# Five FFN pairs with seven block products in place of eight for half of their depth

## What is computed

```python
def swiglu(h, w_ffn_in, w_ffn_out):
    gate, up = jnp.split(h @ w_ffn_in, 2, axis=-1)
    return (jax.nn.silu(gate) * up) @ w_ffn_out
...
        x = x + gate2 * swiglu(h, w_ffn_in[l], w_ffn_out[l])
```

## Time and profile before

| | us |
|---|---|
| median of 3 runs | 3431.92 (3427.52 to 3432.31) |
| profiled execution | 3425.8 |
| its span | 3424.1 |
| TensorE busy | 2587.7 (76%) |
| VectorE busy | 2513.7 (73%) |
| GpSimd busy | 1102.7 (32%) |
| ScalarE busy | 860.9 (25%) |

### The profile page before, as it was taken

The page is one execution under the profiler, slowest core; times in us unless marked ns, Lnnn a source line. Parts: engine busy times, 40 slices in busy tenths (PEclk is TensorE's granted clock), DMA queues, the critical chain, the costliest instruction groups (busy, mean ns, idle before and its releaser), DMA issues. The chain is left out here.

```text
span 3424.1 us, 27357 instructions
## 1 busy us (share of the span) xinstructions
PE 2587.7 (76%) x10431; PEld 1805.0 (53%) x10431; DVE 2513.7 (73%) x2615; ACT 860.9 (25%) x815; POOL 1102.7 (32%) x654
## 2 busy tenths in 40 slices
PE   9999999616051500035558999999999999999999
PEld 4455774202020200012226888788788788888887
DVE  5987657899999999976776876779566544444565
ACT  2113331100000110000003333455433433333333
POOL 6640007686777688876660000000000000000000
PEclk9999999757575755567779999999999999999999
DMA  8885569999999999999997997455657555555775
GB/s 287 320 315 205 183 243 406 403 422 419 422 421 417 409 420 422 422 421 421 422 421 260 327 323 260 145 162 166 221 185 252 167 194 184 192 187 188 269 266 185
DMA packets 317685, 1023.39 MB, mean 299 GB/s; under 512 B 33656, under 2 KB 34184, under 8 KB 250892
## 3 DMA queue, kind: packets, MB, share of 16 engines
q1 hardware_dynamic: 243676, 484.97, 41.2%
q0 software_dynamic: 73904, 537.04, 37.9%
HBM read 1015.08 MB, written 6.86 MB: 298 GB/s over the span
## 5 line engine op out<-in xcount | busy, mean ns | idle before, releaser
L411 DVE TENSOR_TENSOR slab_low<-ring,slab_high 128x2048 fp32r<-128x2048 f32 x220 | 504.2, 2292 | 488.3 <-ACT slab_high L404 488.2
L404 ACT CAST slab_high<-ring 128x2048 fp32r<-128x2048 f32 x284 | 542.3, 1910 | 890.8 <-PE bank L390 714.7
L2137 POOL DMA_INDIRECT pool<-in_peer_u,pool x237 | 493.8, 2084 | 293.5 <-DVE pool L1861 185.9
L1911 DVE CUSTOM_DVE_ANT_0 pool<-pool,nat 128x2048 f32<-128x2048 f32 x234 | 532.7, 2291 | 45.7 <-DMA pool<-in_peer_u,pool 44.2
L388 PE MATMUL bank<-slab_high,left_high 128*128 128x512 f32 x1408 | 551.3, 392 | 8.4 <-DVE res L1949 3.9
L390 PE MATMUL bank<-slab_high,left_low 128*128 128x512 f32 x1408 | 549.0, 390 | 0.0
L389 PE MATMUL bank<-slab_low,left_high 128*128 128x512 f32 x1408 | 548.8, 390 | 0.0
L2710 PE MATMUL bank<-pool,causal 128*128 128x512 f32 x296 | 181.5, 770 | 415.7 <-ACT causal L2352 325.4
L1922 DVE SCALAR_TENSOR_TENSOR res<-pool,res 128x2048 f32<-128x2048 f32 x169 | 397.4, 2351 | 105.9 <-DMA pool<-in_peer_v,pool 92.5
L2137 POOL DMA_INDIRECT pool<-in_peer_v,pool x242 | 394.9, 1632 | 214.0 <-PE bank L2710 107.7
L2710 PE MATMUL bank<-pool,upto 128*128 128x512 f32 x288 | 195.9, 844 | 209.2 <-DMA pool<-in_peer_v,pool 116.3
(11 more groups left out here) (661 smaller groups left out, 3466.1 us busy)
## 6 DMA issues: line engine op xcount, KB each, us to landing
ring<-in_w_in SPq DMA_DIRECT2D x140, 1024.0 KB, 5.2
ring<-in_w_ffn_in SPq DMA_DIRECT2D x88, 1024.0 KB, 5.0
ring<-in_w_ffn_out SPq DMA_DIRECT2D x44, 1024.0 KB, 5.2
nat<-in_w_ada SPq DMA_DIRECT2D x74, 512.0 KB, 5.8
ring<-in_w_out SPq DMA_DIRECT2D x32, 1024.0 KB, 5.1
ring<-in_w_ada SPq DMA_DIRECT2D x28, 1024.0 KB, 6.7
left_scratch<-in_w_ada SPq DMA_DIRECT2D x38, 512.0 KB, 5.7
pool<-in_w_ada SPq DMA_DIRECT2D x12, 1024.0 KB, 7.1
```

The costliest lines, as they stand in the source:

```text
L404: nc.scalar.copy(high[:, n % PARTS], ring[:, g % SLOTS]).then_inc(high_done, 1)
L411: eng.tensor_tensor(dst, ring[:, g % SLOTS], high[:, n % PARTS].bitcast(F32), ALU.subtract)\
L1911: v.tensor_tensor_reduce(out=row, in0=row, in1=nat[:, t, :], scale=1.0, scalar=0.0, op0=ALU.mult, op1=ALU.add, accum_out=actv[:, t, m:m + ...
L2137: g.indirect_dma_start(dst, None, a[table][0], bass.IndirectOffsetOnAxis(idx[:, t, n:n + 1], 0))\
```

## The change

In pairs 1 to 5 the slabs 2 and 3 of the gates and of the ups are taken together. They are a matrix of 2 by 2 blocks (depth chunk 2 or 3, gate or up columns), as are the tokens (tile 0 or 1, depth chunk 2 or 3). The eight block products, 12 matmuls each, become seven by Strassen's scheme with sums of blocks on both sides (Winograd's form, with shared sums). The first two slabs of gates and ups (`rest`) stay as they are and now come behind the seven.

- *Left sums*, once: in pair 0 GpSimd makes four sums of 128x512 from the rows of `nat` (`left_sums`), TensorE turns them (16 transposes), ScalarE and VectorE make the two parts.
- *Weight sums*, each pair: GpSimd makes four sums of 128x2048 in place in the ring (`slab_sums`), each waiting for the one before.
- *Products*: in the order ONE, TWO, THREE, FIVE, SIX, FOUR, SEVENTH, with three part buffers in turn (a third one is added). ONE, TWO, THREE use slabs as loaded; FIVE, SIX, FOUR and SEVENTH use sums 1, 3, 4 and 2.
- *Recombination*: ScalarE takes banks 6 and 7 (ONE, FIVE) to SBUF, VectorE adds in six instructions of 128x512 that read a bank each, GpSimd makes two differences of 128x512 in SBUF, and silu and product work on SBUF tiles (`seven_silu`, `seven_product`).
- *Loads*: each pair still loads eight slabs; first the four for the seven products, then the four rest slabs into the slots in the order 0, 2, 1, 3, when low parts and sums have read them.

Some semaphores of earlier phases are reused in place of new ones, with their counts carried on; these waits are otherwise the same. The core of the diff (the loads and loops of pairs 0 and 6 to 10 do as before):

```diff
+        SEVEN = range(1, 6)
+        tail = 4 * SEVEN.stop * T
...
+        summed_rows = [nat[:, t, n * NB:(n + 1) * NB] for t, n in ((0, 0), (0, 1), (1, 0), (0, 3))]
+        s_wh, s_wl, s_wu = sem("seven_high_parts"), sem("seven_low_parts"), sem("seven_products")
+        s_ws, s_wx, s_wd = sem("slab_sums"), sem("seven_banks_taken"), sem("seven_banks_added")
+        ONE, TWO, THREE, FIVE, SIX, FOUR, SEVENTH = range(7)
+        RING = {ONE: 0, TWO: 1, THREE: 2, FIVE: 0, SIX: 2, FOUR: 1, SEVENTH: 3}
+        PART = {ONE: 2, TWO: 0, THREE: 1, FIVE: 2, SIX: 0, FOUR: 1, SEVENTH: 2}
+        REST_RING, REST_PART = (0, 2, 1, 3), (0, 1, 0, 1)
+        WHICH_SUM = {FIVE: 1, SEVENTH: 2, SIX: 3, FOUR: 4}
+        rest_count = (5, 1, 1, 1)
...
+                def seven_loads(i):
+                    up = i * 8 - 8 + nf
+                    for at, after, p, j in ((0, 5, 0, 2), (2, 7, 1, 3), (1, 7, 0, 3), (3, 8, 1, 2)):
+                        sp.wait_ge(low_done, up + after)
+                        sp.dma_start(ring[:, (gf + at) % SLOTS], ffn_pairs((i, p), j)[0][2]).then_inc(landed[(gf + at) % SLOTS], 16)
+                    for r, (last, sums) in enumerate(((FIVE, 3), (SIX, 4), (FOUR, 4), (SEVENTH, 4))):
+                        at = REST_RING[r]
+                        sp.wait_ge(s_wl, i * 7 - 7 + last + 1)
+                        sp.wait_ge(s_ws, i * 6 - 2 + sums)
+                        sp.dma_start(ring[:, (gf + at) % SLOTS], ffn_pairs((i, r // 2), r % 2)[0][2])\
+                          .then_inc(landed[(gf + at) % SLOTS], 16)
...
+                def left_sums():
+                    g.wait_ge(s_n, len(norm_order))
+                    g.wait_ge(s_nT, turn_order.index((1, 1)) + 1)
+                    x11, x12, x21, x22 = [chunk_of(nat, t, n) for t in range(TT) for n in (2, 3)]
+                    g.tensor_tensor(summed_rows[0], x21, x22, ALU.subtract).then_inc(s_ws, 1)
+                    g.tensor_tensor(summed_rows[2], x11, x21, ALU.subtract).then_inc(s_ws, 1)
+                    g.wait_ge(s_ws, 1)
+                    g.tensor_tensor(summed_rows[1], summed_rows[0], x11, ALU.subtract).then_inc(s_ws, 1)
+                    g.wait_ge(s_ws, 3)
+                    g.wait_ge(s_nT, turn_order.index((3, 0)) + 1)
+                    g.tensor_tensor(summed_rows[3], x12, summed_rows[1], ALU.add).then_inc(s_ws, 1)
+
+                def slab_sums(i):
+                    at = [ring[:, (gf + k) % SLOTS] for k in range(SLOTS)]
+                    g.wait_ge(landed[(gf + 3) % SLOTS], i * 32 + reach[gf + 3])
+                    g.wait_ge(s_wl, i * 7 + (ONE - 6))
+                    g.tensor_tensor(at[0], at[0], at[3], ALU.add).then_inc(s_ws, 1)
+                    g.wait_ge(landed[(gf + 2) % SLOTS], i * 32 + reach[gf + 2])
+                    g.wait_ge(s_ws, i * 6 - 1)
+                    g.tensor_tensor(at[3], at[3], at[2], ALU.add).then_inc(s_ws, 1)
+                    g.wait_ge(s_wl, i * 7 + (THREE - 6))
+                    g.wait_ge(s_ws, i * 6 + 0)
+                    g.tensor_tensor(at[2], at[0], at[2], ALU.add).then_inc(s_ws, 1)
+                    g.wait_ge(s_ws, i * 6 + 1)
+                    g.tensor_tensor(at[1], at[2], at[1], ALU.add).then_inc(s_ws, 1)
+                    g.wait_ge(s_wx, i * 2 + 0)
+                    g.wait_ge(s_wd, i * 4 - 2)
+                    g.tensor_tensor(taken_six, taken_five, taken_six, ALU.subtract).then_inc(s_ws, 1)
+                    g.tensor_tensor(taken_five, taken_five, taken_last, ALU.subtract).then_inc(s_ws, 1)
+
+                left_sums()
+                with g.Fori(SEVEN.start, SEVEN.stop) as i:
+                    slab_sums(i)
...
+                def one_of_seven(i, q, lhs, bank, start):
+                    pe.wait_ge(s_wl, i * 7 + (q - 6))
+                    hi, lo = part_of(PART[q])
+                    for k in range(KS):
+                        lh, ll = lhs(k)
+                        nc.tensor.matmul(ps[bank][:, :], lh, hi[:, k, :], start=start and k == 0, stop=False)
+                        nc.tensor.matmul(ps[bank][:, :], lh, lo[:, k, :], start=False, stop=False)
+                        last = nc.tensor.matmul(ps[bank][:, :], ll, hi[:, k, :], start=False,
+                                                stop=q in (ONE, FIVE, SIX, SEVENTH) and k == KS - 1)
+                    last.then_inc(s_wu, 1)
+
+                def rest(i, r):
+                    p = r // 2
+                    pe.wait_ge(low_done, i * 8 + (nf + 4 + r + 1))
+                    hi, lo = part_of(REST_PART[r])
+                    for k in range(KS):
+                        for t in range(TT):
+                            lh, ll = left(KS * (r % 2) + k, t)
+                            o, end = ps[2 * p + t][:, :], r % 2 == 1 and k == KS - 1
+                            nc.tensor.matmul(o, lh, hi[:, k, :], start=r == 2 and k == 0 and t == 1, stop=False)
+                            nc.tensor.matmul(o, lh, lo[:, k, :], start=False, stop=False)
+                            last = nc.tensor.matmul(o, ll, hi[:, k, :], start=False, stop=end)
+                    last.then_inc(slabs_used, rest_count[r])
+                def seven_pair(i, first):
+                    if first:
+                        pe.wait_ge(s_nl, len(low_order) + 4)
+                    else:
+                        pe.wait_ge(s_wd, i * 4 - 7)
+                    one_of_seven(i, ONE, own(2, 0), 6, True)
+                    pe.wait_ge(s_fa, i * 1)
+                    one_of_seven(i, TWO, own(3, 0), 0, True)
+                    if first:
+                        pe.wait_ge(s_fu, i * 1)
+                    else:
+                        pe.wait_ge(s_wd, i * 4 - 4)
+                    one_of_seven(i, THREE, summed(3), 2, True)
+                    if not first:
+                        pe.wait_ge(s_wd, i * 4 - 6)
+                    one_of_seven(i, FIVE, summed(0), 7, True)
+                    pe.wait_ge(s_wx, i * 2 - 1)
+                    one_of_seven(i, SIX, summed(1), 6, True)
+                    if not first:
+                        pe.wait_ge(s_fl, i * 1 - 1)
+                    hidden_transposes(i)
+                    one_of_seven(i, FOUR, own(3, 1), 1, True)
+                    pe.wait_ge(s_wx, i * 2 + 0)
+                    one_of_seven(i, SEVENTH, summed(2), 7, True)
+                    for r in range(4):
+                        rest(i, r)
...
+                def seven_high(i, q):
+                    at = (gf + RING[q]) % SLOTS
+                    if q in WHICH_SUM:
+                        act.wait_ge(s_ws, i * 6 + (WHICH_SUM[q] - 2))
+                    else:
+                        act.wait_ge(landed[at], i * 32 + reach[gf + RING[q]])
+                    if q == TWO or q == THREE:
+                        act.wait_ge(slabs_used, i * 8 + (gf + (-1 if q == TWO else 0)))
+                    elif q > ONE:
+                        act.wait_ge(s_wu, i * 7 + (q - 9))
+                    elif not isinstance(i, int):
+                        act.wait_ge(s_wu, i * 7 - 7)
+                    dst = third_high if PART[q] == 2 else high[:, (nf + PART[q]) % PARTS]
+                    nc.scalar.copy(dst, ring[:, at]).then_inc(s_wh, 1)
...
+                def take(i, q, bank, into):
+                    act.wait_ge(s_wu, i * 7 + (q - 6))
+                    nc.scalar.copy(into, ps[bank][:, :]).then_inc(s_wx, 1)
...
+                def seven_pair(i):
+                    for q in (ONE, TWO, THREE, FIVE):
+                        seven_high(i, q)
+                    take(i, ONE, 6, taken_one)
+                    for q in (SIX, FOUR, SEVENTH):
+                        seven_high(i, q)
+                    act.wait_ge(s_fu, i * 1)
+                    take(i, FIVE, 7, taken_five)
+                    rest_high(i, 0)
+                    highs(i - 1)
+                    rest_high(i, 1)
+                    rest_high(i, 2)
+                    rest_high(i, 3)
+                    seven_silu(i)
...
+                def one_and_six(i):
+                    dve.wait_ge(s_wx, i * 2 - 1)
+                    dve.wait_ge(s_wu, i * 7 + (SIX - 6))
+                    v.tensor_tensor(taken_six, ps[6][:, :], taken_one, ALU.add).then_inc(s_wd, 1)
+
+                def all_but_five(i):
+                    dve.wait_ge(s_wu, i * 7 + (SEVENTH - 6))
+                    dve.wait_ge(s_wd, i * 4 - 3)
+                    v.tensor_tensor(taken_last, ps[7][:, :], taken_six, ALU.add).then_inc(s_wd, 1)
+
+                def seven_gates(i):
+                    dve.wait_ge(slabs_used, i * 8 + (gf + 6))
+                    dve.wait_ge(s_fT, i * 1)
+                    dve.wait_ge(s_wd, i * 4 - 2)
+                    v.tensor_tensor(prod_[:, 0, :], ps[0][:, :], taken_one, ALU.add)
+                    v.tensor_tensor(prod_[:, 1, :], ps[1][:, :], taken_last, ALU.add).then_inc(s_wd, 1)
+
+                def seven_ups(i):
+                    dve.wait_ge(slabs_used, i * 8 + (gf + 8))
```

(75 more changed lines are left out.)

96 lines of the change are left out of this document (79 added, 17 removed).

## The result

The changed kernel takes **3501.55 us**, median of 4 runs (3501.13 to 3504.80), against 3431.49 for the kernel before on the same chip (4 runs, 3427.52 to 3432.31). The ratio is 1.021, 95% interval 1.0198 to 1.0223: 70 us slower. The profiled execution took 3501.43, span 3499.7. It starts pair 1 at 2731.18 and pair 6 at 3024.51, so the five changed pairs take 293.3 us in place of 222.1.

The account below looks back on a forecast made before the run. TensorE alone was taken to bound pairs 1 to 5; turns between GpSimd and VectorE +60, clock +11 and transposes +1.75 made +73 on 3425.8, or 3499, and 3504 with the median's 6. Range for 8 in 10: 3450 to 3520.

Parts of the forecast that it names:

- What is removed and added on TensorE: TensorE: 60 matmuls fewer over five pairs, 13.6 us; 16 left-sum transposes more in pair 0, 1.75 us.
- The length of a sum: GpSimd's 128x2048 weight sums: 4.5 us each, lower end 3.85, priced from narrower rows.
- The turns: Products of pairs 1 to 5: VectorE and GpSimd instructions alternate whole; TensorE loses 1.2 and 13.9 us a pair, +60 in all.
- What excludes what: VectorE instructions with two SBUF inputs and GpSimd reads exclude each other; VectorE instructions that read a bank keep 0.68 us.
- The clock: TensorE after each 14 us wait: 3.2 to 5.8 us at half rate, 2.3 lost, five times, +11 (8 to 15).
- The first pair: First of the five changed pairs: the product reads banks and takes no turn, so 54.4 us.
- Sum: Whole kernel: 60 + 11 + 1.75 = +73, so 3499 by its own time; the median 6 above it gives 3504.
- No lock: Rival on GpSimd and VectorE: they do not exclude each other, sums still 4.5 us; 3454 to 3462; chance 0.09.
- Sums that hide: Rival on GpSimd's sums: at most 2.6 us each and not kept back, 11.9 us saved, 3420; chance 0.08.
- Kinder turns: Rival on VectorE and GpSimd's order: one 4.5 us turn leaves the path, or only 45.6 a pair; 3440 to 3480; chance 0.14.
- The longer case: Rival on loads and clock: landings at 7.7 us and 5.8 of half clock in several places, 3520; chance 0.05.

Follow-up runs that it names:

- sums of 32 columns: Changed kernel with the four weight sums cut to their first 32 columns, all else kept: 3419.31 us, ratio 0.9966 to the kernel before.
- memsets: Changed kernel with each weight sum replaced by three GpSimd memsets into the same slot, which read nothing from SBUF: 3465.39 us.
- copies: Changed kernel with each weight sum replaced by two GpSimd copies of 128x2048, one SBUF input each: 3485.55 us.
- the filler: Changed kernel with 56 further TensorE matmuls of 512 columns between THREE and FIVE in pairs 2 to 5: 3496.42 us, then 3494.86.
- the kernel with the product later: Changed kernel with seven_product moved on VectorE from ahead of FIVE's low part to behind SIX's: 3498.33 us, then 3496.02.

## Why the prediction was right

3504 was forecast, 3501.55 measured. Step by step:

- **What is removed and added on TensorE** (13.6 less, 1.75 more): the kernel with sums of 32 columns shows 10.9 net (7 to 16 by its interval) against 11.9. The 16 transposes of the left sums took 1.91, with no wait ahead of them, so the four sums on GpSimd before pair 1 are hidden as supposed.
- **The length of a sum** (4.5, lower end 3.85): the shortest listed is 4.51, on the value taken.
- **The turns.** The forecast's schedule, from the start of ONE, against pair 3 (2849.00): sum 1 ends at 4.4 / 4.43, THREE's low part 6.6 / 6.59, sum 2 11.0 / 11.01, sum 3 16.0 / 15.92, sum 4 21.0 / 20.83, FIVE's low part 23.3 / 22.97. The waits were put at 1.2 and 13.9; the rows say 1.0 and 13.3 (over pairs 2 to 5, 1.0 to 2.4 and 13.3 to 13.4). Three places elsewhere in the kernel where both engines meet, carried over to queues that did not exist yet, are what the forecast rests on.
- **What excludes what.** The prediction weighed two pages of the Trainium skill. By the Trainium skill's page Advanced Engine Details and Errata (VectorE Performance Modes), GpSimd is blocked by VectorE's 2-port modes; the low parts and products are, as the prediction has it, no such modes, and they took 4.44, 5.05 and 6.58 in place of 2.29 and 0.68, so that sentence doesn't cover this case. The Trainium skill's page SBUF — State Buffer (Who interferes with whom) says that a VectorE instruction with two SBUF inputs contends with a GpSimd instruction that reads SBUF, and not with one that only writes it. The runs agree on both halves: 2.28 and 0.68 beside memsets, 3.97 and 2.38 beside copies.
- **The clock** (2.3 a pair, 11 in all): FIVE to the transposes took 8.4, 7.8, 7.4 and 7.2 in pairs 2 to 5, and 5.7 to 5.8 with the filler, so 1.4 to 2.7 a pair. In pair 1, FIVE and SIX took 9.95 behind their waits against some 5.7, 4.2 more. That is 12 in all, and its size agrees with the 11; how much of it stays to the end is the 4 to 8 of the filler for four pairs, so the forecast's "nothing after it has slack to absorb it" is not shown.
- **The first pair.** This step was wrong. The forecast has 12.7 lost there (54.4 in place of 41.7) and speaks of one long wait, before FIVE, in each of the five pairs, with distances of 57 to 59; the first distance is 60.9. The timeline of TensorE in pair 1 has two waits, 10.3 together; VectorE's and GpSimd's show why:

```profile
2729.78 4.93 POOL L3618 TENSOR_TENSOR ring<-ring 128x2048 f32<-128x2048 f32 x1 [28.22 <-DMA ring<-in_w_ffn_in]
2731.45 1.28 DVE L4116 TENSOR_TENSOR hidden_rows<-hidden_rows,bank 128x512 f32<-128x512 f32 x2 [1.22 <-PE bank L390]
2736.79 6.67 DVE L4137 TENSOR_TENSOR third_low<-ring,third_high 128x2048 fp32r<-128x2048 f32 x1
2741.45 6.43 POOL L3624 TENSOR_TENSOR ring<-ring 128x2048 f32<-128x2048 f32 x1
2743.51 0.79 PE L3661 MATMUL bank<-third_high,summed_left_high 128*128 128x512 f32 x1 [3.49 <-DVE third_low L4137]
2754.76 0.77 PE L3661 MATMUL bank<-slab_high,summed_left_high 128*128 128x512 f32 x1 [6.76 <-DVE slab_low L4137]
```

  Here the products read a bank: the two of them keep 1.28 together beside sum 1 and take no turn. So FIVE's low part goes before sum 3 (it ends at 2743.46, sum 3 4.4 later), as the forecast's own rule of turns demands, and only SIX's waits for sum 4. FIVE and SIX wait as in the kernel with the product later. The clock made up for the difference by luck: 4.2 behind two waits, where 2.3 was put behind one.
- **Sum.** Five pairs 282 + 11 = 293 forecast, 293.3 measured. That it fits to 0.3 is in part luck: TensorE was idle for 69.7 where the forecast's waits make 73, and busy for 223.6, 15 over its 208.5 (five times 41.7), where the clock was to add 11. The clock rows give 12 of the 15; the other 3 were not traced. Pair 1 starts 4.3 us later than before (2726.90). Of that, 2.6 was there before the left sums came into TensorE's queue (the transposes of the normed rows after VectorE's last wait begin at 2692.37 in place of 2689.72, and the first left sum at 2694.39), which leaves 1.6 for the 1.75 of the transposes. By its own execution the forecast was 3499, where the profile gave 3501.4; the 6 us added for the median did not recur (3501.43 and 3501.55), so that 3504 ended 2.5 high.

The rivals fall as follows. No lock was made true by the memsets: one wait before SIX of 6.3 (5.7 in the rival), 3465 (3454 to 3462). Sums that hide were made true by the 32 columns: 3419 (3420). Kinder turns exist, but the two moved products win 3 to 5 us in the pairs by the traces, not the 20 or more of that rival. The longer case did not come: the loads of this matrix landed in 4.9 us, the median of the page after.

## What to carry to other kernels

Before a second engine is given work because it is idle, ask what the two engines do at the same moment: in these runs, all in float32, a GpSimd instruction that reads SBUF and a VectorE instruction with two SBUF inputs cost the sum of both, and in a chain each pays the other's whole length. A short instruction ahead of an urgent one in the same queue then costs the urgent one as much as the long instruction that it lets in. Price such an overlap from the places in the old trace where both engines already meet, and write the turns out by their ends.

## What was not expected

- A VectorE instruction of 0.68 us can be listed with 5.05, over seven times as long. Busy time does not show it as waiting: VectorE's share looked like work.
- GpSimd's copy of 128x2048 takes 1.90 and its memset 1.81, but the sum of two tiles 4.51, so the sums could not be priced from the copies.
- A wait of 3.5 us can be followed by half rate as one of 13.3 is: in the kernel with the product later FIVE's first matmul in pair 3, after 3.55 idle, is listed with 0.79 as in the changed kernel after 13.33, and the first 4 us have a granted 0.50 in both. It is not always so: in pair 1 of the same trace, after 3.49 idle, it is listed with 0.51 and the first 4 us have a granted 0.57. Cutting one long wait into two therefore won less than the waiting that it removed.
